# A two-block network on one core: its first stage in another order

## The reference

```
h = x @ w_in                                  # columns: u_s5 512 | q 256 | k 256 | v 512 | gate 512
y   = s5 scan of u (32 groups of 16 channels, 64 complex states) + d*u
y   = gelu(y);  y = y * sigmoid(y @ glu_w + glu_b)
y_s5  = y * rsqrt(mean(y^2) + 1e-5) * s5_gain # mean over the 512 channels of a token
y_ret = retention(rotary(q), rotary(k), v)    # 4 heads, decay mask within a chunk, state between chunks
y_ret = groupnorm(y_ret) * gn_gain * silu(gate)
x1 = layer_norm(2**0.25 * x + concat(y_s5, y_ret) @ w_out)
```

## Time and profile before

| | us |
|---|---|
| median of 3 runs | 3431.93 (3431.75 to 3432.1) |
| profiled execution | 3431.33 |
| its span | 3429.5 |
| PE busy | 3127.1 (91% of the span) |
| DVE / ACT / POOL busy | 1222.0 / 896.1 / 1022.5 |
| mean granted TensorE clock | 0.954 of 2.4 GHz |

### The profile page before, as it was taken

The page is one execution under the profiler, slowest core; times in us unless marked ns, Lnnn a source line. Parts: engine busy times, 40 slices in busy tenths (PEclk is TensorE's granted clock), DMA queues, the critical chain, the costliest instruction groups (busy, mean ns, idle before and its releaser), DMA issues.

```text
span 3429.5 us, 35540 instructions
## 1 busy us (share of the span) xinstructions
PE 3127.1 (91%) x14706; PEld 2561.6 (75%) x14706; DVE 1222.0 (36%) x2328; ACT 896.1 (26%) x1321; POOL 1022.5 (30%) x506
## 2 busy tenths in 40 slices
PE   8687799999999979878988888799999999999995
PEld 7566578888888866656776777688887878888884
DVE  8805552221212254455345444402223311111115
ACT  3212323121121133333334444312112411111111
POOL 5214125332232243000431333221222633333332
PEclk9878899999999999988999999999999999999998
DMA  7322212111111112110110010212112111111101
GB/s 177 86 74 92 78 67 62 50 49 62 47 48 48 43 56 82 31 31 31 38 44 32 31 31 31 74 49 74 50 50 98 44 50 62 49 50 50 49 31 49
DMA packets 67248, 192.92 MB, mean 56 GB/s; under 512 B 10288, under 2 KB 18880, under 8 KB 67072
## 3 DMA queue, kind: packets, MB, share of 16 engines
q1 hardware_dynamic: 67088, 190.65, 18.1%
HBM read 165.20 MB, written 25.43 MB: 56 GB/s over the span
## 4 chain that ended last, share of the span: by engine, by line
PE 78%; DVE 6%; ACT 4%; POOL 3%; issue 3%; DMA 1%; SPq 1%; POOLq 0%; DVEq 0%; ACTq 0%
PE PS L365 44%; PE PS L398 7%; PE PS L399 7%; PE PS L400 7%; PE PS L629 3%; PE PS L869 2%; POOL WL L2142 1%; PE PS L758 1%; PE PS L482 1%; PE PS L421 1%; DVE s L1444 1%; POOL DD L2297 1%; PE PS L669 1%; PE PS L670 1%; PE PS L671 1%
## 5 line engine op out<-in xcount | busy, mean ns | idle before, releaser
L2142 POOL TENSOR_TENSOR WL<-WR,WH 128x1024 fp32r<-128x1024 f32 x241 | 576.1, 2398 | 2049.5 <-ACT WH L967 2049.5
L365 PE MATMUL PS<-XH,WH 128*128 128x512 f32 x2176 | 691.4, 399 | 9.8 <-DVE XL L1483 8.9
L365 PE MATMUL PS<-XL,WH 128*128 128x512 f32 x2176 | 677.6, 393 | 0.0
L365 PE MATMUL PS<-XH,WL 128*128 128x512 f32 x2176 | 674.2, 391 | 0.0
L365 PEld LDWEIGHTS PS<-XL,WH 128*128 128x128 f32 x2176 | 414.0, 190 | 88.2
L365 PEld LDWEIGHTS PS<-XH,WH 128*128 128x128 f32 x2176 | 404.9, 191 | 98.5 <-issue 17.8
L365 PEld LDWEIGHTS PS<-XH,WL 128*128 128x128 f32 x2176 | 411.7, 189 | 87.7
L967 ACT ACTIVATE WH<-WR 128x1024 fp32r<-128x1024 f32 x241 | 252.9, 1054 | 782.8 <-PE PS L400 474.6
L398 PE MATMUL PS<-WH,HH 128*128 128x512 f32 x864 | 339.6, 393 | 14.4 <-POOL HL L2174 14.4
L399 PE MATMUL PS<-WL,HH 128*128 128x512 f32 x864 | 338.7, 392 | 0.0
L400 PE MATMUL PS<-WH,HL 128*128 128x512 f32 x864 | 338.3, 392 | 0.0
(11 more groups left out here) (320 smaller groups left out, 3856.8 us busy)
## 6 DMA issues: line engine op xcount, KB each, us to landing
WR<-in_weights SPq DMA_DIRECT2D x241, 512.0 KB, 3.6
spill<-STQ SPq DMA_DIRECT2D x24, 256.0 KB, 2.0
BR<-brbuf SPq DMA_DIRECT2D x12, 512.0 KB, 4.5
RAWX<-in_xT SPq DMA_DIRECT2D x8, 512.0 KB, 7.4
RES<-in_x SPq DMA_DIRECT2D x8, 512.0 KB, 7.2
xbuf<-XF SPq DMA_DIRECT2D x8, 512.0 KB, 2.8
brbuf<-STG SPq DMA_DIRECT2D x8, 512.0 KB, 2.6
RES<-xbuf SPq DMA_DIRECT2D x8, 512.0 KB, 7.9
```

The source lines that it names most:

```text
L365: last = e.matmul(PS[:, u.b + h, :], w, x[:, k, 512 * h:512 * h + 512], start=k == 0 and w is w1 and x is xh, stop=k == nk - 1 and w is w2)
L2142: e.tensor_tensor(WL[:, v % NSPL, :], WR[:, v % NRAW, :], WH[:, v % NSPL, :].bitcast(F), ALU.subtract).then_inc(w_lo, 1)
```

## The change

It reorders the first stage and leaves the rest. The results are the same sums.
- The plan has the two GLU units ahead of the four gate units.
- PE makes the first two kernel products while `prep` is still held, and the other two after one step of `v`. The outputs are spread between the steps of `v`, and all eight steps of `v` are done before the retention begins.
- Each kind of retention product has banks of its own (`at=`): scores 0 and 1, transposes 2, `kv` 3, `outs` 4 and 5, and the large products 6 and 7.
- GLU products 0 and 1 come in step 1 of the retention, 2 and 3 in steps 3 and 4, the gates in steps 2 to 6, and `rt(n-4)` stands at the end of a step, behind the large products.
- The silu of the gates stays on the chip in five buffers `GG`.
- The squares are summed in two passes with one column each per 128 tokens, so the mean is a value per partition; DVE takes the root on 128x8 values, and two matmuls spread it.
- The first half of the output projection runs token step by token step in steps 7 to 11 and behind them, and DVE adds the residual there from its own buffers `RX`.
- DVE makes all nine squarings of the scan's tables in one go, before the coefficient products.

```diff
@@ -61,10 +61,11 @@
 
     for p in range(4):
         feat("w_in", 128 * p)
-    for c in (512, 1024, 1536):
+    for c in (512, 1024):
         tok("w_in", c)
     for c in (0, 256):
         plan.append(("s5_glu_w", 0, 4, c, 256))
+    tok("w_in", 1536)
     for c in (0, 512):
         tok("w_out", c)
...
             qk = pe_token_steps(e, "qk", "w_in", 512, 0, 8, XH, XL, range(8))
-            tick(qk, 6)
+            tick(qk, 5)
             for q in range(4):
                 turn_b(q)
-            tick(qk, 1)
+            tick(qk, 2)
             for q in range(4, 8):
                 turn_b(q)
             finish(qk)
             values = pe_token_steps(e, "v", "w_in", 1024, 0, 8, XH, XL, range(8))
-            bk.let(prep)
             kernel_of(0)
+            kernel_of(1)
             inject(0)
             inject(1)
-            kernel_of(1)
+            bk.let(prep)
+            tick(values, 1)
+            kernel_of(2)
+            kernel_of(3)
             inject(2)
             inject(3)
-            kernel_of(2)
-            tick(values, 1)
-            kernel_of(3)
+            tick(values, 2)
             inject(4)
             inject(5)
             tick(values, 1)
+            outputs(0)
+            tick(values, 1)
             inject(6)
             inject(7)
-            tick(values, 1)
-            outputs(0)
             outputs(1)
             tick(values, 1)
             outputs(2)
             tick(values, 1)
             outputs(3)
+            finish(values)
 
...
+            def squares(m):
+
+                u = claim(e, ("ss", m), at=7)
+                e.wait_ge(g_sq, 2 * m + 2)
+                if m == 0:
                     e.wait_ge(ones_set, 1)
+                for c in range(16):
+                    last = e.matmul(PS[:, u.b, c:c + 1], SG[:, c // 8, 128 * (c % 8):128 * (c % 8) + 128], ones[:, 0:1],
+                                    start=True, stop=True)
+                last.then_inc(u.full, 1)
+
...
+                u = claim(e, "rs", 2, at=6)
...
+                    last = e.matmul(PS[:, u.b + h, :], ones[:, :], SG[:, 0, 512 * h:512 * h + 512], start=True, stop=True)
+                last.then_inc(u.full, 1)
...
+            gates = first = None
             glu_units = []
+            work = {1: ((glu, 0), (glu, 1)),
+                    2: ((gate, 0), (gate, 1)),
+                    3: ((squares, 0), (glu, 2), (gate, 2)),
+                    4: ((glu, 3), (gate, 3)),
+                    5: ((gate, 4), (squares, 1), (gate, 5)),
+                    6: ((gate, 6), (gate, 7), (root, 0)),
+                    7: ((project, 0), (project, 1)),
+                    8: ((project, 2), (project, 3)),
+                    9: ((project, 4),),
+                    10: ((project, 5),),
+                    11: ((project, 6),)}
             for n in range(12):
                 if 1 <= n < 9:
                     scores(n - 1)
                 if 2 <= n < 10:
                     outs(n - 2)
                 if n < 8:
-                    u = claim(e, ("flip", n))
+                    u = claim(e, ("flip", n), at=2)
                     e.wait_ge(r_rot, n + 1)
                     pe_turn_four(e, u, lambda j: QKC[:, n % 2, 128 * j:128 * j + 128])
+                for what, i in work.get(n, ()):
+                    what(i)
                 if 4 <= n:
-                    u = claim(e, ("rt", n - 4))
+                    u = claim(e, ("rt", n - 4), at=2)
                     e.wait_ge(r_y, n - 3)
                     pe_turn_four(e, u, lambda j: YR[:, n % 2, 128 * j:128 * j + 128])
...
+            finish(gates)
+            project(7)
+            finish(first)
...
+            def gate(i):
+                u = lots["g", i]
+                if i in (2, 3):
+                    e.wait_ge(spilled[i % 2], 128)
+                if i >= 5:
+                    e.wait_ge(r_y, i - 4)
+                act_evac(e, u, GG[i % 5][:, :], func=ACT.Silu)
+
+            work = {1: ((sigmoid, 0), (sigmoid, 1)),
+                    2: ((gate, 0), (gate, 1)),
+                    3: ((sigmoid, 2), (gate, 2)),
+                    4: ((sigmoid, 3), (gate, 3)),
+                    5: ((gate, 4), (gate, 5)),
+                    6: ((gate, 6), (gate, 7))}
             for n in range(12):
+                if n < 8:
+                    u = lots["flip", n]
+                    if n >= 2:
+                        e.wait_ge(lots["sc", n - 2].full, lots["sc", n - 2].nfull)
+                        e.wait_ge(r_qx, n - 1)
+                    act_evac(e, u, KQT[:, n % 2, :, :].rearrange("p a c -> p (a c)"))
+                if n == 1:
+                    for p in range(4):
+                        e.wait_ge(tile_in[p], 32)
+                        e.activation(GH[:, p, :], YP[:, p, :], ACT.Copy).then_inc(g_hi, 1)
                 if 3 <= n < 11:
                     i = n - 3
...
+            P0, P1 = L(8), L(9)
+            for k in range(9):
+                then(e.tensor_tensor, L(5), P1, P1, ALU.mult)
+                e.tensor_tensor(L(6), P0, P0, ALU.mult).then_inc(dve, cv.up())
+                then(e.scalar_tensor_tensor, P0, P0, 2.0, P1, ALU.mult, ALU.mult)
+                then(e.tensor_tensor, P1, L(5), L(6), ALU.subtract)
...
+                then(e.tensor_scalar, total, total, 1.0 / 512, EPS, ALU.mult, ALU.add)
+                rsqrt(total, inv, tmp)
...
+            def normed():
+                u = lots["rs"]
+                e.wait_ge(u.full, u.nfull)
+                e.wait_ge(lots["g", 7].full, lots["g", 7].nfull)
+                for p in range(4):
+                    t = e.scalar_tensor_tensor(YP[:, p, :], YP[:, p, :], cols[:, C_GAIN + p:C_GAIN + p + 1], bank(u, 2),
+                                               ALU.mult, ALU.mult)
+                    t.then_inc(g_y, 1)
+                e.wait_ge(g_y, 4)
+                e.tensor_copy(tmp[:, 0:1], PS[:, u.b, 0:1]).then_inc(u.drained, 1)
+                for p in range(4):
+                    e.wait_ge(g_yhi, p + 1)
+                    e.tensor_tensor(XL[:, p, :].rearrange("p (n j) -> p n j", j=8), YP[:, p, :].rearrange("p (j n) -> p n j", j=8),
+                                    XH[:, p, :].rearrange("p (n j) -> p n j", j=8).bitcast(F), ALU.subtract).then_inc(g_ylo, 1)
+
+            outs = {8: (0, 1), 9: (2, 3), 10: (4,), 11: (5,)}
...
             kernel_of(1)
+            sp_spill(e, "v", 0)
             kernel_of(2)
-            sp_spill(e, "v", 0)
             kernel_of(3)
-            e.wait_ge(kt_out[1], 32)
-            e.dma_start(RT[:, :], D["rtab"]).then_inc(cst2, 16)
-            sp_spill(e, "v", 1)
             e.wait_ge(s_t8z, 1)
             for jr in range(8):
                 s = 16 * (7 - jr)
                 e.dma_start(T8[16 * jr:16 * jr + 16, :, s:128], D["ktbuf"][:, :, 0:128 - s]).then_inc(t8_in, 16)
-            for i in (2, 3, 4):
+            e.wait_ge(kt_out[1], 32)
+            e.dma_start(RT[:, :], D["rtab"]).then_inc(cst2, 16)
+            for i in range(1, 6):
                 sp_spill(e, "v", i)
...
             e.wait_ge(s_ss, 4)
             qk(0)
             qk(1)
+            sp_spill(e, "v", 6)
+            s = lots["y8", 3]
             e.wait_ge(s.drained, s.ndrained)
             ybr = D["ybuf"].rearrange("(g c) (j n) -> j c g n", c=16, n=128)
             for j in range(8):
                 e.dma_start(ybr[j], U8[16 * j:16 * j + 16, :, :]).then_inc(yb_out, 16)
-            for n in range(10):
...
+            sp_spill(e, "v", 7)
+            for i in range(3):
+                v(i)
+            e.wait_ge(yb_out, 128)
+            for p in range(4):
+                e.dma_start(YP[:, p, :], D["ybuf"].rearrange("(t p) m -> t p m", p=128)[p]).then_inc(tile_in[p], 16)
+            load(e, lots["v", 7].units)
+            for i in range(2, 8):
+                qk(i)
+                if i == 3:
+                    load(e, lots["glu", 1].units)
+                if i == 6:
+                    load(e, lots["glu", 3].units)
+                if 3 <= i:
+                    v(i)
+            s = lots["glu", 3]
+            e.wait_ge(s.full, s.nfull)
+            for k in range(3):
+                residual(k)
...
             load(e, lots["g", 7].units)
```

More of the change, by code:

```diff
@@ L142, in __init__, with take @@
         self.at = {}
-    def take(self, name, n=1, hold=False, told=True):
-        b = -(-self.turn // n) * n % 8
+    def take(self, name, n=1, hold=False, told=True, at=None):
+        b = -(-self.turn // n) * n % 8 if at is None else at
         while any(x in self.held for x in range(b, b + n)):
             b = (b + n) % 8
-        self.turn = b + n
+        if at is None:
+            self.turn = b + n
         before = {}
@@ L385, in pe_feature, with pe_token_steps @@
                 pass
-        def pe_token_steps(e, name, unit, col, row0, tiles, xh, xl, slots):
+        def pe_token_steps(e, name, unit, col, row0, tiles, xh, xl, slots, banks=None):
```

(62 more changed lines are left out.)

237 lines of the change are left out of this document (96 added, 141 removed).

## The result

| | before | changed |
|---|---|---|
| median, us | 3431.75 (3429.64 to 3432.1, 5 runs) | 3446.05 (3444.8 to 3448.33, 5 runs) |
| profiled execution / its span | 3431.33 / 3429.5 | 3444.88 / 3443.1 |
| mean granted clock | 0.954 | 0.951 |

The ratio is 1.0044 (95% interval 1.0029 to 1.0059): slower by 14 us, where I had forecast 8 us faster and had put the range's end at 3436. Rival D, slower by the slow clock, had 12 in 100.

What follows compares the result with a forecast made beforehand. PE bounds the kernel, so only its idle or slow-clock time can be won. Terms -13.2 + 6 - 1 = -8.2 against 3431.33 gave 3423 us; the forecast's own range was 3416 to 3430, the range over rivals 3405 to 3436.

Steps and rivals of the forecast that it cites:

- Rival D: Outputs 1 to 3 and the retention: the half clock stays, 17 us, so slower at 3440; chance 0.12.
- The first stretch: Start to the last output piece: it ends at 213 instead of 226.2, a term of -13.2 us.
- Item 1: Scan-table squarings in one go: they end some 7 us before the first injection needs them, cost 0 us.
- Item 2: Turns of BB one qk step earlier: the third waits for ACT's copy to STQ, +3.9 us.
- Item 3: Kernel product 0 no longer waits for the scan's tables: -6.5 us.
- Item 4: T's loads go out at 137.6, PE can start output 0 at 152.2, waiting 4.2 us and not 8.1.
- Item 5: Outputs with v steps between, from 152.2: output 0 at half clock takes 15.0; all take 60.6 us.
- rival A: Output 0: the clock rises during it, 6.7 us there and 2.2 in v4, giving 3414; chance 0.18.
- Item 6: Wait for y after the last output: GLU 0 starts 39.5 us later, with 31 us of PE idle.
- Item 7: Waits for the state in retention steps, end of gates and scaling of y before the projection: 45 us.
- Item 8: Slow clock from the last output to the projection's half: 6 plus 7.7, sum 14 us against 27 before.
- its term: Last output piece to the end of the projection's first half: 248 us against 242.0 before, +6.

Runs made afterwards that it cites:

- ACT's cut behind the gates: The changed kernel with ACT's cut of weights after the last gate moved behind the XH of the turned YR: 3444.54 us.
- the kernel with YR between: The changed kernel with the transposes of YR ahead of the last large product of each step, on PE and ACT, not at the step's end: 3400.79 us.

## Why the prediction was wrong

The first stretch and the start of the second came as worked out, or better; the sign was lost in the retention.

- Item 1 held. Item 2 said +3.9 and gave -0.8: ACT was free for STQ at 87.6 and not at 91.2. I had said that no edit moves that moment. It is the landing of a DMA, and it moves by itself: ACT waited for the spill out of STQ until 86.98 here, and until 91.20 in the run "ACT's cut behind the gates", whose code is the same up to there.

```profile
86.98 1.20 ACT L1004 ACTIVATE STQ<-PS 128x512 f32<-128x512 f32 x2 [20.93 <-DMA spill<-STQ]
```

```profile
91.20 1.09 ACT L1004 ACTIVATE STQ<-PS 128x512 f32<-128x512 f32 x2 [24.03 <-DMA spill<-STQ]
```

- Item 3 held: the first two kernel products are one run of 3.68 us from 107.97, with no wait. Item 4 held in its size, 6 us earlier: T's loads at 131.8 (137.6), PE starts at 146.4 (152.2) after 3.0 idle (4.2). Item 5: output 0 took 15.03 at 0.50, as the row of before had it, so rival A fell. The last output ended at 207.5, not 213: the term was -18.7 and not -13.2. Some of that is this one execution's luck: in three experiments with the same code up to there the last output ended at 209.6, 212.1 and 213.2.
- Item 6 held: GLU 0 at 39.9 behind the last output (39.5), with 31.5 idle (31).
- **Item 7 was too small by 7**: 51.6 us of waits and not 45. The five waits for the state are 23.7. The two long ones, 8.58 and 7.20, are where I had 8.6 and 8.3.
- **Item 8 is the step that failed: the slow clock after the change was put at 14 us and is about 29.** It had 6 for the long gaps and 1.1 each for seven small ones. Measured: busy 189.85, less 21 x 5.45 = 114.4, less 46 of small products (36.8, two square sums of 3.63 and one of 1.96), leaves 29 (an estimate, good to some 2 us). Behind GLU 0 there are twelve gaps of 2.25 us or more. Each cost 1.6 to 2.4 where a large product follows (7.3 instead of 5.7) and 0.9 to 2.9 where `outs`, `kv` and a turn do (5.97 us at 0.50 instead of 3.05), together some 23. The two one-column square sums, which the item left out, cost 1.6 each, and the wait for y 3.
- Item 8 also read the kernel before wrongly. It took 0.11 x 242 = 27 us of loss out of a mean clock; that mean counts idle time at the slow clock too, where nothing is lost. Busy 185.8 less 23 large products (125.4) and about 44 of small ones leaves 16. That made the work of before, 159, some 11 too small. But two steps of v (10.9), which the old order has behind the outputs, leave this stretch (ACT spills v 5, 6 and 7 there), and the item did not take them off. So the two errors cancelled by luck, and 159 came near the 161 that the change has. The slow clock went from 16 to 29 and not from 27 to 14.

Of the 25 us by which this stretch came out above its term (+6 said, +30.9 measured), 15 are item 8, 7 are item 7, and 3 are work. The sum by items, with what was measured: -18.7, then idle 56.2 to 83.1 (+26.9), slow clock +13, work less by two steps of v (-10.9) and more by the square sums (+1.7), -1.7 at the second half; this makes +10.3 from rounded terms, against 10.5 in the trace.

Rival D named the mechanism and its place only in part: outputs 1 to 3 ran at the full clock (8.42 each), the slow clock came in the retention alone. That the waits and the clock together were the position of `rt(n-4)` is shown by the run in which only that is moved, with ACT's part of it: 45 us.

In the prediction I weighed the Trainium skill's page "TensorE: Matmul & The Clock Gate" (section "What's actually happening"), by which activity releases the slow clock, against the earlier trace rows. The runs side with the row: output 0 started slow stayed slow for 15.03 us of unbroken products, and the same products started fast ran 8.4 us at 1.00. The same section of the Trainium skill has the slow clock as the state after idle time, and there the trace agrees: with the waits filled with transposes the clock from 324 to 470 was 0.98 and not 0.79.

## What to carry to other kernels

Price a small gap in front of PE by what follows it, not by its own length alone: in the changed kernel the waits of 2.25 to 8.6 us cost another 0.9 to 2.9 us each in slow products, and the longest did not cost the most. So a reorder that merges large products and leaves short waits between them can lose what it gains. When transposes feed ACT, then DVE, then PE again, put one large product between them and their reader. And take the loss by slow clock from busy time less the known price of the products, never from a stretch's mean clock, which counts idle time.

## What the hardware showed that I had not expected

- Square sums of one column (32 products in 3.63 us, PE busy throughout) left the slow clock behind them as a wait does: the gate step behind them took 7.34 and not 5.7, after only 0.45 of idle time. The GLU product after 1.30 us of idle time between large products took 5.68, the full clock. With no idle time at all the sums did it too: in the kernel with YR between, the second pass and the transposes right behind it have

```profile
331.99:336.19 4.20, 4.20 (x33) 4.20 (x32) 3.48 (x10) 1.49 (x5) 1.98 (x3) 0.82 0.02 4
336.19:337.25 1.06, 1.06 (x5) 0.69 (x5) 0.93 (x3) 0.50 (x2) 0.00 (x0) 0.50 0.00 0
```

- A wait of one length does not have one price. Behind the second wait for the state, 3.42 us in both, the same six groups of products ran at the half clock in the changed kernel and at the full clock in the run "ACT's cut behind the gates". In the kernel before, two waits of 2.65 us in front of scores were followed by 3.37 us at 1.00 and by 5.02 at 0.66.

```profile
351.47:357.38 5.91, 5.91 (x21) 5.08 (x21) 5.26 (x26) 0.00 (x0) 0.37 (x1) 0.50 0.00 0
```

```profile
354.64:357.69 3.05, 3.05 (x20) 2.79 (x21) 2.64 (x13) 0.00 (x0) 0.11 (x1) 1.00 0.00 0
```

- Idle transposes of a 128x128 identity, 0.12 us each, were enough to hold the full clock through waits of 3 to 9 us. One kernel gained 11.6 us and another 7.5 from work whose results nobody reads.
